# A backward forget projection made of seven half-size products, with conditioning sums 1024 wide and two small moves in the attention steps

## The reference: what is computed

```python
mod = split(silu(c) @ w_ada + b_ada, 6)            # conditioning: shifts, scales, gates, 6 x 1024
h_lat = modulate(rmsnorm(x, g_mix), mod[0], mod[1])
h_ctx = modulate(rmsnorm(ctx, g_mix), mod_c[0], mod_c[1])
zl, zc = split_in(h_lat @ w_in), split_in(h_ctx @ w_in)
def forget(f_raw, lower):                          # f_raw: ff (forward) or fb (backward)
    f = lower + (1 - lower) * sigmoid(f_raw)
    return 1 - f, log(f)
# hgrn2: two gated linear scans (forward with ff, backward with fb) over context, then latent tokens
b_lat = rmsnorm(o_lat, hg_norm_g) * silu(zl[7])     # the read-out
# grouped attention: queries and keys are normed: rmsnorm(q), rmsnorm(k), then rotated
y_lat = branch_merge((a_lat, b_lat, c_lat), zl[11:14], w_branch, w_out)
x = x + mod[2] * y_lat
x = x + mod[5] * hierarchical_moe(modulate(rmsnorm(x, g_ffn), mod[3], mod[4]))   # 16 experts, top 2
return rmsnorm(x, g_final)
```

## Time and profile before

| | |
|---|---|
| median of 3 runs | 690.83 us (689.97 to 695.64) |
| the profiled execution: its time, its span | 689.49 us, 687.7 us |
| busy: PE, DVE, POOL, ACT | 671.4, 353.5, 303.2, 101.7 us |
| granted TensorE clock over the span | 0.997 of full speed |
| bytes moved | 183.78 MB, 267 GB/s on average |

### The profile page before, as it was taken

The page is one execution under the profiler, slowest core; times in us unless marked ns, Lnnn a source line. Parts: engine busy times, 40 slices in busy tenths (PEclk is TensorE's granted clock), DMA queues, the critical chain, the costliest instruction groups (busy, mean ns, idle before and its releaser), DMA issues.

```text
span 687.7 us, 9089 instructions
## 1 busy us (share of the span) xinstructions
PE 671.4 (98%) x3720; PEld 448.0 (65%) x3720; DVE 353.5 (51%) x576; ACT 101.7 (15%) x182; POOL 303.2 (44%) x182
## 2 busy tenths in 40 slices
PE   9999999999999998999999999999999999999996
PEld 5344588998989566788888988666535534434432
DVE  3459694869741689877666634346203203203214
ACT  4011112111001221311111240012000000000003
POOL 0029999999999799795544200000000000000014
PEclk9999999999999999999999999999999999999998
DMA  9992555051344653433492269866999999999993
GB/s 353 417 408 98 216 226 198 33 187 59 122 154 179 249 214 155 182 124 123 153 386 89 79 274 434 345 256 216 414 418 423 420 421 421 422 420 421 419 415 148
DMA packets 29515, 183.78 MB, mean 267 GB/s; under 512 B 3543, under 2 KB 5975, under 8 KB 14624
## 3 DMA queue, kind: packets, MB, share of 16 engines
q1 hardware_dynamic: 27456, 178.72, 65.1%
q0 software_dynamic: 1584, 3.97, 1.5%
q10 hardware_dynamic: 432, 0.49, 0.2%
HBM read 178.15 MB, written 6.82 MB: 269 GB/s over the span
## 4 chain that ended last, share of the span: by engine, by line
PE 81%; DVE 10%; DMA 5%; ACT 2%; issue 2%; POOL 1%; SPq 0%; DVEq 0%; POOLq 0%
PE bank L1488 21%; PE bank L973 18%; PE bank L954 6%; PE bank L937 6%; PE bank L1244 4%; PE bank L933 4%; PE bank L1446 4%; PE bank L960 3%; PE bank L1190 2%; PE bank L1065 2%; PE bank L1167 2%; DVE sb L1851 2%; DMA sb<-y_rows 1%; PE bank L1175 1%; DMA y_rows<-sb,token_rows 1%
## 5 line engine op out<-in xcount | busy, mean ns | idle before, releaser
L1488 PE MATMUL bank<-sb 128*64 128x512 f32 x768 | 166.8, 594 | 0.7 <-ACT sb L866 0.7
L973 PE MATMUL bank<-sb 128*128 128x128 f32 (+1 forms) x1008 | 152.2, 311 | 1.0 <-DVE sb L1736 1.0
L973 PEld LDWEIGHTS bank<-sb 128*128 128x128 f32 x1008 | 139.3, 192 | 11.1 <-issue 3.0
L718 POOL DMA_INDIRECT y_rows<-sb,token_rows x7 | 7.0, 1003 | 268.1 <-DVE sb L2119 268.1
L1488 PEld LDWEIGHTS bank<-sb 128*64 128x64 f32 x768 | 54.3, 137 | 106.5 <-issue 103.8
L2079 DVE TENSOR_TENSOR sb<-sb,bank 128x512 f32<-128x512 f32 x8 | 5.5, 688 | 98.9 <-PE bank L1488 98.9
L672 POOL TENSOR_TENSOR sb<-sb 128x1024 f32<-128x1024 f32 x24 | 47.8, 1990 | 4.9 <-DMA sb<-ada_w 3.1
L1736 DVE TENSOR_TENSOR sb<-bank,sb 128x256 f32<-128x256 f32 (+1 forms) x63 | 32.3, 512 | 26.2 <-PE bank L973 21.6
L1676 DVE COPY sb<-bank 128x512 f32<-128x512 f32 x45 | 29.2, 682 | 31.0 <-PE bank L1120 12.8
L937 PE MATMUL bank<-sb 128*128 128x256 f32 x192 | 42.1, 380 | 0.0
L954 PE MATMUL bank<-sb 128*128 128x256 f32 x192 | 41.9, 380 | 0.0
(11 more groups left out here) (264 smaller groups left out, 875.7 us busy)
## 6 DMA issues: line engine op xcount, KB each, us to landing
sb<-expert_w SPq DMA_DIRECT2D x90, 1024.0 KB, 17.5
sb<-front_w SPq DMA_DIRECT2D x19, 2048.0 KB, 8.7
sb<-ada_w SPq DMA_DIRECT2D x32, 512.0 KB, 3.6
sb<-ada_mix SPq DMA_DIRECT2D x4, 2048.0 KB, 20.4
sb<-expert_w SPq DMA_DIRECT2D x12, 512.0 KB, 10.5
sb<-xcT SPq DMA_DIRECT2D x4, 512.0 KB, 6.4
sb<-front_w SPq DMA_DIRECT2D x4, 512.0 KB, 21.2
y_rows<-sb SPq DMA_DIRECT2D x4, 512.0 KB, 23.4
```

The source lines that it names most:

```text
L973: ins = pe.matmul(o, left, right, start=(k == 0), stop=(k == 3))
L1488: ins = pe.matmul(bank[e * CAP:(e + 1) * CAP, :], lhsT[:, k, e * CAP:(e + 1) * CAP], weights_at(k, e), start=(k == 0), stop=(k == parts - 1))
```

## The change

1. `fb` joins the projections made of seven products. Its 32 matmuls of 512 columns become 56 of 256. POOL makes four sums for it: three before everything else once the weights have landed (`weight_sums("fb")`), the last before part q = 3. The first `x_sums` waits for half of `h_ready` instead of all of it; `fourth` now waits until `sums_ready` is 4. DVE adds the seven products before its four scalings for `fb`, which go by heads 2, 3, 0, 1; ACT takes the sigmoid in four pieces from memory. PE waits for `mix_out` and for banks of `ff` where `fb` now begins, and `hq` waits for sums of `fb`.
2. Conditioning sums: a group's first part is multiplied into `ada_acc` (1024 elements), each later one is multiplied in place and added to it in one addition of 1024; one addition of 512 closes the group (L699 of the changed kernel). Three waits move there; the sum of group 9 lies elsewhere.
3. ACT makes the squares of `gq` and of the keys as it takes them out of the banks; DVE keeps the two reductions, the keys' being one for both halves at the end of step 3. `gqa_norms` goes ahead of `normalise` in step 4.
4. `o_scaled` is parted: `o_divided` (1024 elements) in step 2, the rest (1024) in step 3.
5. SP's loads of `b_rows` and `row5`, and the wait for `b_ready` ahead of them, move from behind the load of `gate2` to before it.

```diff
-SEVEN = ("hi", "nk", "nv") + GATES
+SEVEN = ("fb", "hi", "nk", "nv") + GATES
...
         w_sums = {"hi": [at(A0 + 1024 * i, 4, L) for i in range(2)]}
+        w_sums["fb"] = w_sums["hi"]
...
+                if name == "gate2":
+                    sp.wait_ge(b_ready, 1)
+                    sp.dma_start(b_rows, d["b_rows"][:, 0:2, :]).then_inc(brow_in, 16)
...
-            pool.wait_ge(h_ready, KD)
-            link(pool.tensor_tensor(x_sums[0], x_part(0, 1), x_part(0, 0), ALU.subtract))
...
+            pool.wait_ge(mix_ready, 1)
+            weight_sums("fb")
+            pool.wait_ge(h_ready, KD // 2)
+            link(pool.tensor_tensor(x_sums[0], x_part(0, 1), x_part(0, 0), ALU.subtract))
+            pool.wait_ge(h_ready, KD)
+            link(pool.tensor_tensor(x_sums[1], x_part(1, 1), x_sums[0], ALU.subtract))
...
             for q in range(PARTS * len(POOLED)):
+                if q == 3:
+                    last_weight_sum("fb")
...
+                scaled = ada_acc if first_part else w
...
-                link(last)
-                if k0 == 0:
-                    ins = pool.tensor_tensor(ada_sum[g], w[:, 0, :], w[:, 1, :], ALU.add)
-                else:
-                    link(pool.tensor_tensor(w[:, 0, :], w[:, 0, :], w[:, 1, :], ALU.add))
-                    ins = pool.tensor_tensor(ada_sum[g], ada_sum[g], w[:, 0, :], ALU.add)
...
+                if not first_part:
+                    link(last)
+                    last = pool.tensor_tensor(ada_acc, ada_acc, w, ALU.add)
...
+                    pool.tensor_tensor(ada_sum[g], ada_acc[:, 0, :], ada_acc[:, 1, :], ALU.add).then_inc(ada_summed, 1)
...
-                    act.activation(gq[:, i, :], ps[:, :], ACT.Copy).then_inc(done, 1)
+                    act.activation(gq[:, i, :], ps[:, :], ACT.Copy)
+                    act.activation(g_sq[:, 512 * i:512 * i + 512], ps[:, :], ACT.Square).then_inc(done, 1)
...
-            for n in range(4, fill_no("hg", 1)):
+            first("fb")
+            fourth("fb")
+            second("fb")
+            sixth("fb")
+            seventh("fb")
+            fifth("fb")
+            third("fb")
+            for n in range(fill_no("hq"), fill_no("hg", 1)):
...
             for dr in range(2):
-                name = ("ff", "fb")[dr]
-                for h in range(HGH):
+                if dr:
+                    sums_of_first("fb")
+                    sums_of_seventh("fb")
+                    sums_of_fifth("fb")
+                    sum_of_third("fb")
+                for h in ((0, 1, 2, 3), (2, 3, 0, 1))[dr]:
...
+            def o_divided():
+                dve.wait_ge(o_rec, 2)
+                dve.tensor_tensor(o_sb, o_sb, o_tmp, ALU.mult).then_inc(o_rec, 1)
...
-                link(dve.tensor_tensor(g_sq[:, 0:1024], q, q, ALU.mult))
```

More of the change, by code:

```diff
@@ L87, in operand_no @@
 def operand_no(name, last):
+    if name == "fb":
+        return (0, 1, 2, 3, 5)[last]
     return 1 + (name in GATES) + 4 * SEVEN.index(name) + last
@@ L129, in emptied @@
     who = FILLS[n][2]
-    return who, (7 if who == "sums" else 1) * sum(f[2] == who for f in FILLS[:n + 1])
+    done = (7 if who == "sums" else 1) * sum(f[2] == who for f in FILLS[:n + 1])
+    return who, done + (FB_GATES if who == "act" and n > fill_no("fb") else 0)
 UNITS = [(k, t, c) for k in ("na", "gq") for t in range(NT) for c in range(4)]
@@ L540, in _ @@
                     sp.dma_start(na_bias, d["na_bias"]).then_inc(bias_in, 16)
-                if name == "gate2":
-                    sp.wait_ge(b_ready, 1)
-                    sp.dma_start(b_rows, d["b_rows"][:, 0:2, :]).then_inc(brow_in, 16)
-                    sp.dma_start(row5.rearrange("p (a b) -> p a b", a=2), d["b_rows"][:, 2:4, :]).then_inc(row5_in, 16)
                 if name == "br2":
@@ L765, in fill @@
                 done = out_by["act"]
-                if name in ("ff", "fb"):
-                    act.activation(forget[:, :, 4 * (name == "fb") + i, :], two, ACT.Sigmoid).then_inc(done, 1)
+                if name == "ff":
+                    act.activation(forget[:, :, i, :], two, ACT.Sigmoid).then_inc(done, 1)
                 elif name in ("hq", "hg"):
@@ L791, in copy_first @@
                 act.activation(out_part(name, 0, 0), product_out(name, 1), ACT.Copy).then_inc(part_copied, 1)
-            for n in range(fill_no("nq")):
+            for n in range(fill_no("fb")):
+                fill(n)
+            copy_first("fb")
+            for last, fh, th in ((2, 0, 0), (4, 1, 0), (5, 1, 1), (7, 0, 1)):
+                act.wait_ge(out_by["sums"], sums_no("fb", last))
+                act.activation(out_part("fb", fh, th), out_part("fb", fh, th), ACT.Sigmoid).then_inc(out_by["act"], 1)
+            for n in range(fill_no("hq"), fill_no("nq")):
                 fill(n)
@@ L922, in fill @@
                     wait_emptied(pe, before[-1])
+                if name == "hq":
+                    pe.wait_ge(out_by["sums"], sums_no("fb", (1, 4)[i]))
                 if name == "gq":
@@ L930, in fill @@
                     take_slot(g)
-                if name == "fb":
-                    for k in range(KD):
-                        ins = pe.matmul(ps[:, :], lhs(w, k, i * P), hT[:, k, :], start=(k == 0), stop=(k == KD - 1))
-                elif name in ("hq", "hg", "nq"):
+                if name in ("hq", "hg", "nq"):
                     for c in range(2):
@@ L1638, in _, with add_product, sums_of_first, sums_of_seventh @@
             link(dve.tensor_scalar(span, lower, -1.0, 1.0, ALU.mult, ALU.add))
-            for dr in range(2):
-                name = ("ff", "fb")[dr]
-                for h in range(HGH):
+            out_sums = out_by["sums"]
+            def add_product(name, step, m, dst, src):
+                if m == 3 or (m == 5 and name in GATES):
+                    dve.wait_ge(fill_ready, multiplied(name))
+                else:
+                    dve.wait_ge(part_ready, product_no(name, 7 if m == 6 and name in GATES else m))
+                if step > 1:
+                    dve.wait_ge(out_sums, sums_no(name, step - 1))
+                dve.tensor_tensor(out_part(name, *dst), product_out(name, m), out_part(name, *src), ALU.add).then_inc(out_sums, 1)
+            def sums_of_first(name):
+                dve.wait_ge(part_copied, SEVEN.index(name) + 1)
+                add_product(name, 1, 6, (0, 1), (0, 0))
+                add_product(name, 2, 2, (0, 0), (0, 0))
+            def sums_of_seventh(name):
+                add_product(name, 3, 7, (1, 1), (0, 1))
+                add_product(name, 4, 4, (1, 0), (1, 1))
+            def sums_of_fifth(name):
+                add_product(name, 5, 5, (1, 1), (1, 1))
+                add_product(name, 6, 5, (0, 1), (0, 1))
+            def sum_of_third(name):
+                add_product(name, 7, 3, (0, 1), (0, 1))
+            for dr in range(2):
+                if dr:
[4 more added lines that the diff above has]
+                for h in ((0, 1, 2, 3), (2, 3, 0, 1))[dr]:
                     j = dr * 4 + h
-                    dve.wait_ge(out_by["act"], emptied(fill_no(name, h))[1])
+                    if dr == 0:
+                        dve.wait_ge(out_by["act"], emptied(fill_no("ff", h))[1])
+                    else:
+                        dve.wait_ge(out_by["act"], emptied(fill_no("ff", 3))[1] + (3 if h > 1 else 4))
                     ins = dve.tensor_scalar(forget[:, :, j, :], forget[:, :, j, :], span[:, j:j + 1],
```

96 lines of the change are left out of this document (42 added, 54 removed).

## The result

The changed kernel takes 695.79 us in the median of 20 runs (693.47 to 697.99), the kernel before 691.82 of 20 beside it. The ratio is 1.0055, 95% interval 1.0041 to 1.007: about 3.8 us slower, where 1.8 less was forecast.

What follows compares the result with a forecast made beforehand. PE, busy 671.4 of 687.7 us, was taken as the bound nearly everywhere. Terms +1.2 (front) and -3.0 (attention steps) gave -1.8: 689.5 becomes 687.7, forecast as a median of 689.0, range 684.3 to 695.2.

Steps and rivals of the forecast that it cites:

- Part 1, the products and the features: Front up to `level(0)`: a saving of 3.3 from the products less waits of 3.4 and 1.1, sum +1.2 us.
- `kc_ready` 105.0: End of DVE's chain for the context keys: ready at 105.0, PE there at 103.9, so PE waits 1.1.
- the premise of the forecast: Late scans of DVE's chain to `kc_ready`: POOL's TENSOR_SCALARs do not hold DVE up; three scans at 0.55 each.
- rival B: Context keys: TENSOR_SCALARs also hold DVE up, scans take 1.9 and more, PE waits 6.7; total 694.6 us; chance 0.20.
- the feature wait: Near 48.7 in `ff`: POOL's early sums delay DVE's last features, so PE waits 3.4 us.
- Parts 3 and 4: Attention steps: less DVE work in step 2 removes PE's waits of 3.2 but for 0.2; sum -3.0 us.
- Under the 1024-wide additions the two L1851 of a step can be held up by a little more each, and I leave 0.2 of the waits standing: Attention steps: wider POOL additions delay DVE's divisions only slightly, costing 0.2 us of the 3.2 to be gained.
- the 0 to 1 for part 2: Wider conditioning sums, rounds of `level`: 0, at most 1 us either way; a group about 1 us shorter on POOL.
- A shift at `level(0)` and at step 4 carried to the end unchanged: All after step 5 is paced by PE or moves with it, so shifts at both places reach the end unchanged.
- Part 5: Loads of `b_rows` moved earlier: land before step 4 asks near 280; cost 0, at worst no more than 4.5 us.
- C: Attention steps: parts 3 and 4 gain only 1, each L1851 held up by up to 2.2; total 691.0 us; chance 0.13.
- A's clean gain: Front: DVE goes first, features in time, `kc_ready` at 101, part 1 gives -2.8; total 684.8 us; chance 0.22.

Runs made afterwards that it cites:

- e3: The kernel before with the seven half-size products of `fb` alone; ratio 1.0091.
- e4: The changed kernel with its conditioning sums 512 wide again, all other edits kept; ratio 1.0002.
- e5: The changed kernel with POOL's conditioning parts of steps 0 to 2 held behind DVE's divisions, and gate0's weight sums behind L1850; 691.43 us, ratio 0.9982.
- e10: The changed kernel with the holds of e5, and POOL's gate0 and gate1 weight sums held behind DVE's divisions of steps 4 and 6; 687.48 us, ratio 0.9932.
- e13: The changed kernel with dummy PE products: 7 before the turns of steps 1 and 3, 1 in step 2, 6 in step 6; 694.40 us, ratio 1.001.
- e8: The changed kernel with each 1024-element addition of a conditioning part cut into two of 512; 692.48 us, ratio 0.9999.
- e1: The kernel before with only the attention steps' edits (squares on ACT, `o_scaled` parted, step order, `b_rows` loads); 688.46 us, ratio 0.9953.
- e2: The kernel before with only the conditioning sums added 1024 wide; ratio 1.0091.
- e6: The changed kernel with POOL's four input sums put ahead of the weight sums of `fb`; 700.58 us, ratio 1.0102.
- e14: e10 with two weight sums of `fb` ahead of the features, then the input sums once all features are done, then the third weight sum; 687.41 us, ratio 0.9919.
- e11: The changed kernel with dummy PE products: 15 before the turns of steps 1 and 3, 3 in step 2, 14 in step 6; 697.47 us, ratio 1.0072.

## Why the prediction was wrong

**Part 1, the products and the features: right, but for one term.** Forecast: the wait 3.4, the products 24.2, `kc_ready` 105.0, a wait of 1.1, `level(0)` +1.2. Measured: 2.90; 24.34; L1742 done at 103.59; no wait; +0.72. POOL stood idle for 1.17 before one part, which the chain did not foresee: two of the four scans took only 0.68 there, the third met an ordinary part (2.30), and only the fourth and L1742 met TENSOR_SCALARs:

```profile
100.17 1.10 DVE L1739 TENSOR_TENSOR_SCAN sb<-sb 128x255 f32<-128x255 f32 x1
101.30 2.29 DVE L1742 TENSOR_TENSOR sb<-sb 128x2048 f32<-128x2048 f32 x1
...
99.79 5.23 POOL L684 TENSOR_SCALAR sb<-sb 128x512 f32<-128x512 f32 x2
```

The fourth scan ended at 101.26, before the first of the two TENSOR_SCALARs did (101.60), so it did not wait that one out: the premise of the forecast held, on little evidence, and the sign of rival B (1.9 and more) did not come. The term that is missing is the clock: in the profiles of e3, e4, e5, e10 and e13 the feature wait, 2.6 to 3.8, is followed by a lower granted clock, the rows of the `ff` matmuls behind it take 8.54 to 8.83 instead of 7.13, and `level(0)` is 2.2 to 3.3 late (in e3 with a wait of 1.08 at the context keys). The profiled execution of the changed kernel escaped it (2.90), as did e8 (3.08); that its +0.72 lies under the forecast is in part this luck.

**Parts 3 and 4: the size was right when nothing else moved.** e1 gives -3.3 by its ratio for a forecast of -3.0; in its profile PE is 3.14 ahead at the turn of step 3, as forecast, and 1.94 at step 7.

**The step that failed** is "Under the 1024-wide additions the two L1851 of a step can be held up by a little more each, and I leave 0.2 of the waits standing", with the 0 to 1 for part 2. It priced the turns that the divisions had before, not the ones they would have once POOL's work fell elsewhere (in step 0 it began at 233.6, ahead of the division, instead of 235.5, behind it). The working of part 2 hid this: a group of conditioning sums became some 2.5 shorter, not 1, so POOL's work did not stay where it was (in e2, with this edit alone, its part in step 0 began at 232.3). In the profile the pairs went from 0.88 to 3.49 in step 0, from 2.39 to 4.19 in step 2 and from 2.98 to 4.83 in step 6; PE waits 6.4 in the five rows above, against 3.7 in the same places before (3.2 in the earlier trace rows and 0.46 in step 6), and the clock behind them adds 1.6 in `gkv`'s fill and 0.95 in the scores of step 6. From `level(0)` to step 7 PE so lost 6.7, where the forecast had it gain 3.0. e5 and e10 take these waits away by place alone: 0.73% and 0.50% by the ratios, some 8 us together.

**"A shift at `level(0)` and at step 4 carried to the end unchanged"** holds from step 7 on (PE's lag is +7.39 at 316 and at its last matmuls; the other 1.1 of the spans' 8.5 comes behind them, and why was not looked into), but not in the steps: a shift changes which POOL instruction a division meets. The list of PE rows taken as the bound hid this. **Part 5** cost nothing, as forecast: the loads went out at 274.7 and landed 4.0 to 4.8 later, and nothing waited for them.

**The rivals.** C named the right engines and instruction and put them at +0.2; the price of a turn was 2, in more steps than it counted, and with the clock on top. B gave nearly the measured time (694.6) by luck: nothing waited at the context keys. That wait does exist once the feature wait is cured (3.21 in e6, 3.45 in e14), so A's clean gain was not there in any order tried.

The Trainium skill, page "SBUF — State Buffer", section "Who interferes with whom", says that the shared ports are locked for a whole instruction, that TENSOR_SCALAR can be among those that lock them, and that it is the order of issue that decides who blocks. The rows of the divisions agree: L1894 has one input in memory and takes 0.49 alone, and 2.0 to 2.6 where it had to wait out nearly the whole of a 1024-element instruction of POOL; the first of step 4, which began 0.3 ahead of POOL's, took 0.49.

## What to carry to other kernels

Where VectorE and GpSimd both touch memory, price each short VectorE instruction on the path by the GpSimd instruction that it will meet, at its new place, and if it meets one, hold GpSimd behind a semaphore that VectorE's step already sets: here six such waits were worth 8 us, more than all that the change was to save. And when a helper engine's work is reshaped, take the price of its new instruction from a row of the same kind, for it sets where all its later work falls. Before halving a product on TensorE, follow the other engine's chain to the next point where TensorE needs it: the 3.3 us saved were lost there or at the features. Try the parts of a change one by one: this one held a gain of 0.5%, two losses of 0.9%, and with the holds a version at 0.9885.

## What the runs showed that was not expected

- Behind some PE waits of 1.8 to 3.8 us the granted clock fell, and behind others as long it did not (2.61 in e3 against 2.90 in the changed kernel and 3.08 in e8, all at the features). Executions of one kernel differ likewise in their mean clock, and the time goes with it in the main: 693.70 at 0.999, 697.63 at 0.991. With small products in the waits of the steps the profiles show 1.00 there (e11, e13).
- Such a dummy, 128x128 in f32 with its own weights, took 0.24, two records each.
- VectorE and GpSimd took turns in the steps: in the changed kernel each division that found a GpSimd addition or product under way ended 0.28 to 0.35 after it. Work added to GpSimd can delay a load, too (`na_bias`, by 5 us in e4).
- Of VectorE and GpSimd it was GpSimd that gave way where it ran a TENSOR_SCALAR: the two behind 99.79 in the changed kernel took 1.81 and 3.42 (1.56 at the shortest elsewhere), while VectorE's scan and product beside them took 1.10 and 2.29, little over their own time.
